# RWKV recurrence: block-diagonal 128x128 products or pairs of 64x64 products on two quarters of the array

## What is computed

```python
def step(S, inp):
    r_t, d_t, k_t, v_t, kk_t, b_t = inp
    sa = -jnp.einsum('bhij,bhj->bhi', S, kk_t)
    S = S * d_t[:, :, None, :] + sa[..., None] * b_t[:, :, None, :] + v_t[..., None] * k_t[:, :, None, :]
    return S, jnp.einsum('bhij,bhj->bhi', S, r_t)
S_last, y = lax.scan(step, wkv0, (rh, dh, kh, vh, kk, bh))
```

## Time and profile before

| | us |
|---|---|
| device time, median of 3 runs | 1630.89 |
| lowest and highest run | 1630.31, 1639.07 |
| span of the profiled execution | 1634.1 |
| the 8 turns of the recurrence loop within it | about 333.97 to 960.70 |
| PE matmul busy | 1526.2 (93%) |
| PE weight loads busy | 985.8 (60%) |
| DVE busy | 741.2 (45%) |
| ACT busy | 341.8 (21%) |

### The profile page before, as it was taken

The page is one execution under the profiler, slowest core; times in us unless marked ns, Lnnn a source line. Parts: engine busy times, 40 slices in busy tenths (PEclk is TensorE's granted clock), DMA queues, the critical chain, the costliest instruction groups (busy, mean ns, idle before and its releaser), DMA issues.

```text
span 1634.1 us, 20748 instructions
## 1 busy us (share of the span) xinstructions
PE 1526.2 (93%) x8005; PEld 985.8 (60%) x8005; DVE 741.2 (45%) x1394; ACT 341.8 (21%) x633; POOL 205.6 (13%) x316
## 2 busy tenths in 40 slices
PE   8999999999999999999999999999999398978975
PEld 5888666577777777777777865666444232322322
DVE  5655199942534444536343433577744401101116
ACT  3001211411313131322313136000122111101113
POOL 3008300022110111111010010100000010101100
PEclk9999999999999999999999999999999599989998
DMA  7101011032221322121113121474300779675648
GB/s 219 52 26 52 13 34 37 26 134 87 79 68 39 117 49 78 34 72 48 53 35 121 52 93 43 151 287 168 135 39 26 265 263 348 235 273 198 223 168 324
DMA packets 47235, 194.70 MB, mean 119 GB/s; under 512 B 6408, under 2 KB 6904, under 8 KB 42400
## 3 DMA queue, kind: packets, MB, share of 16 engines
q1 hardware_dynamic: 28144, 116.13, 20.4%
q0 software_dynamic: 18992, 77.25, 13.1%
HBM read 353.23 MB, written 41.44 MB: 242 GB/s over the span
## 4 chain that ended last, share of the span: by engine, by line
PE 85%; DMA 5%; DVE 4%; issue 2%; SPq 2%; ACT 2%; POOL 0%; DVEq 0%; POOLq 0%; ACTq 0%
PE ps L549 29%; PE ps L617 7%; PE ps L897 7%; PE ps L946 6%; PE ps L1046 6%; PE ps L1060 4%; DMA arena<-in_w_gu 3%; PE ps L841 3%; PE ps L755 2%; PE ps L750 2%; PE ps L760 2%; PE ps L733 2%; SPq L476 1%; PE ps L564 1%; DMA scr<-h_rows,idx 1%
## 5 line engine op out<-in xcount | busy, mean ns | idle before, releaser
L549 PE MATMUL ps<-arena,wring 128*128 128x344 f32 x1728 | 528.5, 452 | 0.6 <-DVE arena L1472 0.6
L549 PEld LDWEIGHTS ps<-arena,wring 128*128 128x128 f32 x1728 | 314.4, 189 | 143.5 <-issue 1.9
L1046 PE MATMUL ps<-arena,scr 128*32 128x512 f32 x1280 | 150.6, 617 | 19.2 <-DMA arena<-in_w_gu 19.0
L2122 POOL DMA_DIRECT2D gate_scratch<-stage x96 | 52.1, 544 | 617.0 <-ACT stage L1186 544.2
L897 PE MATMUL ps<-arena,wring 128*128 128x344 f32 x384 | 111.2, 451 | 0.0
L1046 PEld LDWEIGHTS ps<-arena,scr 128*32 128x32 f32 x1280 | 39.4, 112 | 114.2 <-issue 82.0
L897 PEld LDWEIGHTS ps<-arena,wring 128*128 128x128 f32 x384 | 72.5, 189 | 38.6
L1060 PE MATMUL ps<-arena,scr 128*32 128x512 f32 x640 | 77.7, 628 | 14.6 <-issue 13.2
L1186 ACT ACTIVATE stage<-ps 128x344 f32<-128x344 f32 x84 | 38.4, 457 | 253.2 <-PE ps L549 253.1
L2006 DVE TENSOR_TENSOR scr<-scr,ps 128x256 f32<-128x256 f32 x20 | 8.4, 421 | 180.8 <-ACT scr L1369 180.8
L1703 DVE TENSOR_TENSOR scr<-scr,ps 128x512 f32<-128x512 f32 x40 | 27.5, 688 | 127.9 <-PE ps L755 127.9
(11 more groups left out here) (450 smaller groups left out, 2125.7 us busy)
## 6 DMA issues: line engine op xcount, KB each, us to landing
arena<-in_w_gu SPq DMA_DIRECT2D x336, 512.0 KB
arena<-in_w_dn SPq DMA_DIRECT2D x80, 1024.0 KB
wring<-in_w_all SPq DMA_DIRECT2D x55, 512.0 KB, 3.7
gate_scratch<-stage POOLq DMA_DIRECT2D x96, 172.0 KB, 2.2
arena<-gate_scratch POOLq DMA_DIRECT2D x4, 2064.0 KB, 9.2
scr<-gate_scratch POOLq DMA_DIRECT2D x4, 2064.0 KB, 9.2
arena<-y_rows SPq DMA_DIRECT2D x16, 512.0 KB, 9.7
arena<-in_w_out SPq DMA_DIRECT2D x2, 2048.0 KB, 15.9
```

The lines of the kernel that those rows point to most:

```text
L549: mm = pe.matmul(ps[:, c, 0:CW], wring[:, slot, k, :], H[:, k, chunk(c)], start=k == 0, stop=k == KT - 1)
L1046: mm = pe.matmul(ps[S * j:S * (j + 1), i % 2, :], XT[i % 2][:, k * P + S * j:k * P + S * (j + 1)], GU[j][:, k * 2 * HID:(k + 1) * 2 * HID] ...
L2122: pool.dma_start(gate_scratch[:, g:g + 1, chunk(c)], stage[:, c:c + 1, :]).then_inc(sem(f"gate_out{c}"), 16)
```

## The change

The block-diagonal copies, their memsets, both `spread` functions and the semaphores `kr` and `bkv` go. A helper `blocks` makes each product as a pair of 64x64 products, one per head: rows and weights columns 0 to 63 for the first, 64 to 127 for the second, both into the same PSUM bank on their own partitions. Operands are read in place from `kk`, `bb` and `PR`, and all results and masks are 64 columns wide instead of 128. The transposes become such products against a stacked 64x64 identity (`eye64`). The products of line 733 are split in two (kk and r are no longer adjacent). In the state step the two head pairs share one semaphore, one DVE operation and one PSUM bank per stage. The fillers, their number and their places are the same. The two accumulated products of the SSM output (817, 818) are issued in another order. The constants are 576 columns smaller on balance.

```diff
+                def blocks(dst, left, right, start=True, stop=True):
+                    for h in HEADS:
+                        mm_ = pe.matmul(dst[h, :], left[h, :], right[h, :], start=start, stop=stop)
+                    return mm_
...
-                pe.wait_ge(sem("kr"), i + 1)
-                pe.wait_ge(sem("bkv"), i + 1)
...
                 for q in range(4):
-                    mm = pe.matmul(ps[:, 3, q * P:(q + 1) * P], KR[:, q, 0, :], BT[:, q, :], start=True, stop=True)
+                    mm = blocks(ps[:, 3, q * RC:(q + 1) * RC], k_of(i, q), b_of(i, q))
                 mm.then_inc(sem("prod"), 1)
-                for n in range(4):
-                    for q in range(2 * (n % 2), 2 * (n % 2) + 2):
-                        mm = pe.matmul(ps[:, 4 + n, (q % 2) * 256:(q % 2) * 256 + 256], (BT if n < 2 else KTB)[:, q, :],
-                                       KR[:, q, :, :].rearrange("p a b -> p (a b)"), start=True, stop=True)
+                for n, left in enumerate((lambda q: b_of(i, q), lambda q: rkv_of(S_K, i, q))):
+                    for q in range(4):
+                        blocks(ps[:, 4 + n, 2 * q * RC:(2 * q + 1) * RC], left(q), k_of(i, q))
+                        mm = blocks(ps[:, 4 + n, (2 * q + 1) * RC:(2 * q + 2) * RC], left(q), rkv_of(S_R, i, q))
                     mm.then_inc(sem("prod"), 1)
...
-                        mm = pe.transpose(ps[:, 3 + n, q * P:(q + 1) * P], src[:, q, :], ident)
+                    mm = blocks(ps[:, 3, q * RC:(q + 1) * RC], rkv_of(S_V, i, q), eye64)
...
-                        mm = pe.matmul(ps[:, 6, q * P:(q + 1) * P], NLB[:, q, :], U[:, q, :], start=True, stop=True)
+                        mm = blocks(ps[:, 6, q * RC:(q + 1) * RC], NLB[:, q, :], U[:, q, :])
...
-                        mm = pe.matmul(ps[:, 7, q * P:(q + 1) * P], TT[:, q, :], X1[:, q, :], start=True, stop=True)
+                        mm = blocks(ps[:, 7, q * RC:(q + 1) * RC], TT[:, q, :], X1[:, q, :])
...
-                    ins_ = tt(U, U, ps[:, 7, :].rearrange("p (a b) -> p a b", a=4), SUB)
+                    ins_ = tt(U, U, ps[:, 7, 0:4 * RC].rearrange("p (a b) -> p a b", a=4), SUB)
...
-                    for t in range(2):
-                        act.wait_ge(sem("yy"), 4 * i + 2 * c2 + t + 1)
-                        A(tick[:, 2 * c2 + t:2 * c2 + t + 1], cst[:, 0:1], ACT.Copy)
-                        for h in range(2):
-                            ins_ = A(PR[64 * h:64 * h + 64, S_R + t:S_R + t + 1, bass.ds(i * SC + c2 * RC + PAD, RC)],
-                                     ps[64 * h:64 * h + 64, 6 + t:7 + t, 64 * h:64 * h + 64], ACT.Copy)
-                        ins_.then_inc(sem("y_ev"), 1)
+                    act.wait_ge(sem("yy"), 2 * i + c2 + 1)
+                    o = i * SC + c2 * RC
+                    A(rows(S_R, 2, o, o + RC), ps[:, 6:8, 0:RC], ACT.Copy).then_inc(sem("y_ev"), 1)
```

More of the change, by code:

```diff
@@ L745, in _ @@
+                mm.then_inc(sem("turned"), 1)
                 filler(2)
@@ L765, in _ @@
                 for c2 in range(2):
+                    pe.wait_ge(sem("st"), 2 * i + c2 + 1)
                     for t in range(2):
                         q = 2 * c2 + t
[L768 to L775, removed]
+                        blocks(ps[:, 4, t * RC:(t + 1) * RC], k_of(i, q), ST[:, t, :], stop=False)
+                        mm = blocks(ps[:, 4, t * RC:(t + 1) * RC], MK[:, q, 0, :], VT[:, q, :], start=False)
@@ L785, in _ @@
[L785 to L790, removed]
+                        blocks(ps[:, 4, t * RC:(t + 1) * RC], BTT[:, q, :], SA[:, t, :], stop=False)
@@ L791, in _ @@
+                        blocks(ps[:, 4, t * RC:(t + 1) * RC], KTT[:, q, :], VT[:, q, :], start=False, stop=False)
+                        mm = blocks(ps[:, 4, t * RC:(t + 1) * RC], eye64, ST[:, t, :], start=False)
+                    mm.then_inc(sem("ss"), 1)
+                    for t in range(2):
+                        mm = blocks(ps[:, 6 + t, 0:RC], SA[:, t, :], BM[:, 2 * c2 + t, 1, :], start=False)
+                    mm.then_inc(sem("yy"), 1)
                     filler(1)
@@ L813, in _ @@
                 pe.wait_ge(sem("btok"), i + 1)
[L814 to L818, removed]
+                pe.wait_ge(sem("y_ev"), 2 * i + 2)
+                for g in range(2):
+                    for left, right in ((XDT, EE), (HT, EA)):
+                        for h in range(2):
+                            mm = pe.matmul(ps[HEADS[h], 7, g * P:(g + 1) * P], left[:, g, HEADS[h]], right[:, 2 * g + h, :],
+                                           start=left is XDT, stop=left is HT)
                 mm.then_inc(sem("sy"), 1)
@@ L1195, in _, with turn @@
             act.wait_ge(sem("pre_done"), 1)
-            def spread(i):
-                for w, src in enumerate((kk, PR)):
-                    for h in range(2):
[L1200 to L1206, removed]
+            def turn(i):
                 g0 = G_PRE + sum(G_TURNS[:i])
@@ L1253, in turn @@
                     A(DA_S, DA_S, ACT.Exp).then_inc(sem("pre_act"), 1)
-                if more:
-                    spread(i + 1)
                 filler(FILLS)
-            spread(0)
             gate_chunk(0, 2)
-            for i in range(0, NITER - 1):
-                turn(i, True)
-            turn(NITER - 1, False)
+            for i in range(0, NITER):
+                turn(i)
             act.wait_ge(sem("st_out"), 32)
@@ L2188, in sample_second, with turn @@
                         pool.dma_start(outs["ssm_h"][:, t], ssm_h[:, t, :, 1:]).then_inc(sem("small_out"), 16)
-            def turn(i, more):
+            def turn(i):
                 g0 = G_PRE + sum(G_TURNS[:i])
                 for j in range(G_TURNS[i]):
-                    if j == 1 and more:
-                        pool.wait_ge(sem("turned"), 3 * i + 3)
-                        spread(i + 1)
                     gate_store(g0 + j)
@@ L2200, in turn @@
                         sample_second(i)
-            spread(0)
             gate_store(0)
-            for i in range(0, NITER - 1):
-                turn(i, True)
-            turn(NITER - 1, False)
-            pool.wait_ge(sem("ssm_fin"), 2 * NITER + 2)
+            for i in range(0, NITER):
+                turn(i)
+            pool.wait_ge(sem("ssm_fin"), 2 * NITER)
             out("wkv_p", ST, "st_out")
```

178 lines of the change are left out of this document (93 added, 85 removed).

## The result

The changed kernel takes 1587.8 us (median of 4 runs, 1586.1 to 1589.8) against 1630.8 us before. The ratio is 0.972, 95% interval 0.969 to 0.975. The prediction was 1584 us, 1572 to 1618.

The account below looks back on a forecast made before the run. TensorE's order was taken to bound the loop: 12.30 us gross minus 6.66 for shape changes, 5.64 per turn, 45.1 in 8 turns, plus 2 from a stall, 47 in all. Forecast 1584 us from the median, range 1572 to 1618.

Parts of the forecast that it names:

- Which engine bounds the loop: Recurrence loop: a microsecond of TensorE's order is a microsecond of the kernel, as long as no gap opens.
- The short instruction: The 64x64 products: 27.9 ns per instruction with two quarters at once; 496 per turn cost 13.84 us, against 26.14 removed.
- The change of shape: Between full-array fillers and quarter groups: 0.37 us in and out together, 18 times per turn, 6.66 us.
- Transposes and line 779: Two groups that lose: transposes from 1.30 to 1.34 + 0.37 us, line 779 from 0.44 to 0.22 + 0.37.
- The stall before line 796: TensorE's wait of 5.4 us in 8 turns: about a third, 2 us, gained, with 0 and 5 as ends.
- No overlap: Rival, all 496 short instructions: halves run one after the other, 55.8 ns each, 66 us slower, 1697 us; chance 0.11.
- Dearer changes or issue: Rival, quarter groups: 0.55 us per shape change (1612 us) or 35.6 ns per instruction (1616), chance 0.14; both 1642, 0.03.
- Gaps: Rival, loop: shorter groups leave 0.31 us idle at each of 18 places, gain gone, 1631 us; chance 0.05.
- Clock: Rival, loop: quarter groups run at half clock, adding 13.8 us per turn, 1694 us; chance 0.03.
- the prediction's own sign: Loop: a clock under 1.00 inside it would make the prediction wrong.
- The rule of the page: Pairs writing one PSUM bank: by the rule the halves run one after the other; the prediction weighed lines 817's overlap more.
- The total: Whole kernel: 45.1 + 2 = 47 us off, 1587 us from the profiled span, 1584 from the median; chance 0.64.

Follow-up runs that it names:

- tiles_alone: Kernel before with only the 128x128 products split into 64x64 pairs in turns 1 to 7, DVE and ACT operations still 128 wide: 1594.4 us, ratio 0.973.
- best: Kernel after with transposes right behind the first products, one filler share moved to the turn's end, ACT's gate evacuation behind the SSM's sigmoid: 1577.4 us, ratio 0.965.
- same_quarter: Kernel after, turns 1 to 7: both products of each non-accumulated pair are the first head's, on the same quarter of the array: 1671.9 us.
- after_again: The changed kernel unaltered, run once more on the same chip as best: 1586.5 us, ratio 0.970.
- rows_only: Kernel after, five levels: both products of a pair use the same array columns, only row halves differ, results in different banks: 1604.1 us, one run.
- one_shape: Kernel after, fourth turn only: fillers and recurrence products all 128 rows by 64 columns, paired on column halves: 1587.2 us, one run; that turn 60.89 us.

## Why the prediction was right

- **Which engine bounds the loop.** Right: 48.3 us left the loop, PE's busy time fell by 48.4, and tiles_alone gave 41.9 us in seven turns with all other engines' operations as before. In the same stretch the kernel after gained 41.3.
- **The short instruction.** I took 27.9 ns from lines 817 and 818; measured 29.1. The small error is the step "half of 111 ns for half the columns": alone on a quarter it is 58 and not 55.8 ns. 496 of them cost 14.4 us and not 13.8.
- **The change of shape.** I took 0.37 us; measured 0.345. 18 visits cost 6.2 us and not 6.7. That the two errors cancel is luck: 20.6 us added per turn, 20.5 forecast, and 5.62 us gained in a 4-tile turn, 5.64 forecast.
- **Transposes and line 779.** Right in sign: the transposes take 1.54 + 0.195 us and took 1.30, line 779's group 0.38 + 0.195 and took 0.44.
- **The stall before line 796.** Forecast 2 us of 5.4 gone, measured 1.8. The number is right and the mechanism was incomplete: the wait vanished in the five 3-tile turns (0.36 each there), where ACT's copies of y lead the chain (with the six small copies, in tiles_alone, it stayed). It stayed at 1.2 in the three 4-tile turns, where ACT has a gate evacuation in front of the sigmoid (in the third turn of the kernel after at 563.45, the sigmoid at 563.80). In best, where that evacuation stands behind the sigmoid, the wait is gone.
- **What I left out.** The 3-tile turns gained 6.51 us. Besides the 5.5 and the wait of 0.36, a visit right behind a wait doesn't pay the 0.195 us in front: the first group of a turn starts after 0.59 us of waiting. The remaining 0.45 us is nearly all in the timelines. The stretch from the filler before line 796 to the end of the transposes behind it takes 4.41 us (631.70 to 636.11) and took 4.95 (653.81 to 658.76), 0.54 less and not 0.36. The list counts a wait's idle time from the end of a record, but without the wait the next group would have started before that end. Lines 817 and 818 in the new order take 1.02 us and not 1.07. The last filler and the wait at the end of a turn take 1.91 and not 2.00, and the first group of before takes 4.42 behind its wait and 4.34 without one. The first turn gained about 7 us; part of it runs at half clock (3.4 us in both kernels, from 331.3 before and from 332.4 after).
- **The rivals.** No overlap: refuted by same_quarter, which shows what it would have cost. Dearer changes or issue: both prices came out near the values taken. Gaps: DVE's gap in a level grew from 1.23 to 1.60 us, so the cover is larger than before. Clock: in the profile of the kernel after the granted clock is 1.00 in the loop from 336 us on. In after_again it fell once, from 658.9 to 662.3 us, to 0.50 (1.2 of 2.4 GHz), after PE had idled for 1.90 us (the rows below). So the prediction's own sign, a clock under 1.00 inside the loop, did appear behind the first turn in one of two profiles. It came behind a wait and not with the quarter groups, and it cost 1.7 us once, not 13.8 per turn.
- **The rule of the page.** The Trainium skill, TensorEngine Tiling (Array Packing), section Restrictions and Gotchas, says that row tiles cannot access one PSUM bank simultaneously. The trace does not agree for two quarters that differ in both rows and columns: in the same bank a group of 16 takes 0.61 us, as in rows_only in different banks. The rule's plainest case, two row halves on the same columns and in one bank, was not tried.
- **The total.** 47 us forecast; 48.0 in the profiled spans, 43.0 between the medians. I went from the span to the median by the 3.2 us of the kernel before; the profiled span of the kernel after stands 1.7 below its median instead. So the forecast for the span, 1587, was 0.9 us off and the one for the median, 1584, was 3.8 off. The spread of the runs (1586.1 to 1589.8, before 1630.3 to 1639.1) covers the difference; by the interval of the ratio the gain is 41 to 51 us.

One thing stays open. In the fifth turn of the kernel after, PE waits once for ACT's copy of the first level, 0.6 us in one profile and 1.9 us in after_again, where ACT stood idle for 4.09 us. In after_again the clock falls behind it, and the 8 fillers from 658.73 take 4.20 us and not 2.51:

```profile
657.21 0.38 ACT L1249 ACTIVATE scr<-ps 128x256 f32<-128x256 f32 x1 [4.09 <-remote]
657.65 1.15 PE L745 MATMUL ps<-scr 64*64 64x64 f32 x32 [1.90 <-ACT scr L1249]
658.73 4.27 PE L566 MATMUL ps<-arena,wring 128*128 128x344 f32 x8
662.93 0.68 PE L745 MATMUL ps<-scr 64*64 64x64 f32 x16
```

So this turn takes 70.27 us there, 67.30 in the kernel after and 66.61 without the wait. PE had finished the product that ACT copies by 654.4. The profile names no engine as what released ACT ("remote"), and no run here tells what it was. In both profiles a 16 KB transfer of an instruction queue starts in the gap, at 654.10 and at 653.44 us. That ACT waited for instructions would fit this, but such transfers start every 7 to 18 us in this part of the loop, so it may be chance.

## What to carry to other kernels

Splitting a block-diagonal product into quarters nearly doubles its rate here (0.116 us and not 0.223 for a 128x128 block), but each visit to another shape between full-array work costs about a third of a microsecond, here more than half of the gross gain; count visits before instructions, and merge groups where a bank allows it. Alternate the quarters from product to product, since an instruction for the free quarter started ahead of three waiting ones and not of eight. The larger prize is one shape for all work of a stretch: the fourth turn in 128x64 halves throughout was 5.7 us shorter, from which I estimate 46 us for the loop. It would need weights that are zero in the other head's rows, as in the block-diagonal copies of the kernel before; no kernel here does that.

## What was not expected of the hardware

Two products overlap fully when only their row halves differ, or only their column halves (0.61 us for 16 instructions in each case). A change between half and quarter shape costs about as much as one from the full array: with half fillers a group of 16 takes the same 0.61 us and the filler stretch in front loses about 0.15 us (2.47 against 2.31 in one_shape). The same 128x344 filler as two column halves costs the same as one whole (2.31 us for 16 halves, 2.32 for 8 wholes).
